# Context before tokens at the ends of feed-forwards, a later silu, and GpSimd's sums of a gate on VectorE

## The reference

```python
for l in range(2):
    m  = (silu(c)     @ w_mod[l] + b_mod[l])      # 9 vectors of 1024: shift, scale, gate of three sublayers
    mc = (silu(c_ctx) @ w_mod[l] + b_mod[l])      # the same for the context
    x  = x  + 0.5 * m[2]  * swiglu(mod_norm(x,  m,  0), w1, w2)      # feed-forward "a", width 2816
    xc = xc + 0.5 * mc[2] * swiglu(mod_norm(xc, mc, 0), w1, w2)
    h, hc = mod_norm(x, m, 1), mod_norm(xc, mc, 1)
    # mixers: convolution, pooling, neighbourhood attention of h over itself and hc's keys and values;
    # in layer 0 hc is mixed too, in layer 1 only its keys and values are needed
    x = x + m[5] * (mixers(h, hc) @ w_out);  xc likewise in layer 0
    x = x + 0.5 * m[8] * swiglu(mod_norm(x, m, 2), w3, w4)           # feed-forward "b"; xc only in layer 0
return rms_norm(x, final_g)
# mod_norm(x, m, i) = rms_norm(x, g) * (1 + m[3i+1]) + m[3i]
# swiglu(h, w1, w2) = (silu(a) * b) @ w2 with a, b = split(h @ w1)
```

## Time and profile before

| | us |
|---|---|
| median of 3 runs | 3647.82 (3643.95 to 3649.64) |
| profiled execution, its own time | 3641.98 |
| its span, first to last instruction | 3640.1 |

### The profile page before, as it was taken

How to read it: one execution, slowest core, us unless ns; L and a number is a source line. 1 busy time by engine, 2 the same in 40 slices (tenths; PEclk the granted TensorE clock), 3 DMA queues, 4 the chain that set the end, 5 groups by cost and what they waited for, 6 DMA issues and landing times.

```text
span 3640.1 us, 45778 instructions
## 1 busy us (share of the span) xinstructions
PE 3329.7 (91%) x17814; PEld 2927.8 (80%) x17814; DVE 2582.4 (71%) x4566; ACT 1320.5 (36%) x2339; POOL 806.9 (22%) x773
## 2 busy tenths in 40 slices
PE   6989799998899997999789999878999979889998
PEld 4778678786899996877679999868999968778886
DVE  4476668786889887465598888878988863653333
ACT  3465442323333334334433333343333343332222
POOL 0000011112433330301063333234333303100000
PEclk9999999999999998999899999989999989999999
DMA  3201245462233332522113333222333324113332
GB/s 124 90 24 41 76 139 184 141 190 73 79 104 105 110 105 80 157 89 75 44 50 105 110 105 102 90 67 87 102 105 101 103 88 121 47 59 98 93 99 76
DMA packets 382857, 348.89 MB, mean 96 GB/s; under 512 B 17344, under 2 KB 338240, under 8 KB 382128
## 3 DMA queue, kind: packets, MB, share of 16 engines
q1 hardware_dynamic: 337600, 250.74, 22.8%
q10 hardware_dynamic: 29088, 52.57, 4.6%
q0 software_dynamic: 15952, 42.65, 3.9%
HBM read 339.60 MB, written 2.10 MB: 94 GB/s over the span
## 4 chain that ended last, share of the span: by engine, by line
PE 49%; DVE 36%; ACT 8%; issue 6%; DMA 1%; POOL 0%; ACTq 0%; DVEq 0%; SPq 0%; POOLq 0%
PE ps L765 47%; DVE lob L2242 5%; DVE Tm L2846 5%; DVE MRa L2265 5%; ACT hib L1507 3%; DVE MRb L2265 3%; DVE X L2416 2%; ACT Tm L1507 2%; DVE lob L2240 2%; PE ps L768 1%; DVE Tm L2355 1%; DVE Gla L2855 1%; DVE Hl L2366 1%; DVE C L2416 1%; DVE ACC L2332 1%
## 5 line engine op out<-in xcount | busy, mean ns | idle before, releaser
L765 PE MATMUL ps<-Hh,hib 128*128 128x512 f32 (+2 forms) x2624 | 959.1, 366 | 83.3 <-DVE lob L2242 42.7
L765 PE MATMUL ps<-Hl,hib 128*128 128x512 f32 (+2 forms) x2624 | 942.2, 359 | 0.0
L765 PE MATMUL ps<-Hh,lob 128*128 128x512 f32 (+2 forms) x2624 | 941.9, 359 | 0.0
L2240 DVE TENSOR_TENSOR lob<-rawb,hib 128x1024 fp32r<-128x1024 f32 (+3 forms) x355 | 437.2, 1235 | 474.1 <-ACT hib L1507 472.8
L1507 ACT ACTIVATE hib<-rawb 128x1024 fp32r<-128x1024 f32 (+2 forms) x595 | 510.4, 865 | 670.5 <-PE ps L765 542.0
L765 PEld LDWEIGHTS ps<-Hh,hib 128*128 128x128 f32 x2624 | 507.4, 193 | 161.5 <-DVE lob L2242 51.4
L765 PEld LDWEIGHTS ps<-Hh,lob 128*128 128x128 f32 x2624 | 506.7, 193 | 51.7
L765 PEld LDWEIGHTS ps<-Hl,hib 128*128 128x128 f32 x2624 | 508.0, 194 | 49.9 <-issue 2.0
L765 PE MATMUL ps<-Gha,hib 128*128 128x512 f32 (+1 forms) x704 | 243.0, 345 | 9.4 <-ACT Tm L1507 4.0
L2265 DVE CUSTOM_DVE_ANT_0 MRa<-MRa 128x512 f32<-128x512 f32 x256 | 249.0, 1017 | 0.0
L765 PE MATMUL ps<-Gha,lob 128*128 128x512 f32 (+1 forms) x704 | 241.1, 342 | 0.0
(11 more groups left out here) (314 smaller groups left out, 6233.9 us busy)
## 6 DMA issues: line engine op xcount, KB each, us to landing
rawb<-in_ffn_w_in SPq DMA_DIRECT2D x120, 512.0 KB, 3.9
rawb<-in_ffn_w_out SPq DMA_DIRECT2D x88, 512.0 KB, 3.4
rawb<-in_w_in SPq DMA_DIRECT2D x74, 512.0 KB, 3.7
rawb<-in_w_ff SPq DMA_DIRECT2D x64, 512.0 KB, 3.6
MRa<-in_w_mod_t ACTq DMA_DIRECT2D x128, 256.0 KB, 2.7
rawb<-in_ffn_w_in SPq DMA_DIRECT2D x112, 256.0 KB, 3.2
MR<-in_w_mod_t POOLq DMA_DIRECT2D x96, 256.0 KB, 3.4
MRb<-in_w_mod_t ACTq DMA_DIRECT2D x64, 256.0 KB, 2.7
```

The costliest lines, as they stand in the source:

```text
L765: return e.matmul(out, lhsT, rhs, start=start, stop=stop)
L2240: e.tensor_tensor(lob_of(x.chunk), raw_of(x.chunk), hib_of(x.chunk), ALU.subtract).then_inc(*done(("lo", x.u)))
```

## The change

- At a last part's end the context's four pairs come first, then the tokens'; the context's norm runs in turn beside the tokens' pairs, in groups 1, 1, 4, 4 (`NORM_BY_4`). `following` names the context's norm, and every `ffn` opens with the tokens' norm between. The weights' order follows (`residual`, `sweeps`).
- The mixers open with the context's values, in layer 0 its three convolution products too, and the tokens' norm runs in turn beside them (`NORM_OPENING`); the tokens' values and the keys come behind.
- For the token norms 0, 2, 3, 5, 6, 8, 9 (`alone`) DVE doesn't add the last two squares to ACC: PE sums them straight from Tm. DVE's X updates of a pair come before its sums. The diagonals are signalled, and spread, one by one.
- `silu(turn)` moves from the start of `ffn` to behind its first pair (DVE waits for it before a row).
- `seven`: ACT's copy of product 5 and POOL's two adds go; DVE makes `b1` and `b2` from `u` and product 5 in PSUM. The last gate and its high and low half (`gated a2`, `high a2`, `low a2`) are put behind the first units of the next pair, except in a part's last pair.
- Rows: turns of 56, 56, 58, 59, 59; three behind an output chunk, and one at position 4 of every second crossed pair. In ACT's `gemm` the halves come before the row DMAs.

```diff
-        for some in ([[s] for s in sets] if apart else [sets]):
+        for some in ([[s] for s in sets[::-1]] if apart else [sets]):
...
+        tm(("v2", l, "c"), w, 8, 2048, 512, 2)
         if l == 0:
             conv("c")
+        tm(("v2", l, "x"), w, 8, 2048, 512, 4)
+        for pair in range(2):
+            fm(("k2", l, pair), w, 8, [1536 + 256 * pair, 1664 + 256 * pair], ["x", "c"])
...
+def alone(s, n):
+
+    return s == "x" and n in (0, 2, 3, 5, 6, 8, 9)
...
 NORM_BY_4, NORM_BY_8 = (1, 1, 4, 4), (1, 1, 2, 2, 2, 2)
+NORM_OPENING = [(0, 1, 0, 1, 1, 1, 1, 1, 2, 2), (0, 1, 1, 2, 6)]
...
-        mod_turns = [(0, 0, 48, 2, 0), (0, 48, 48, 2, 0), (0, 96, 64, 2, 2), (1, 16, 64, 2, 2), (1, 80, 64, 2, 2)]
+        mod_turns = [(0, 0, 56, 2), (0, 56, 56, 2), (0, 112, 58, 3), (1, 26, 59, 3), (1, 85, 59, 3)]
...
                     for i in range(nt // 128):
-                        m = mm(ps[:, b, i:i + 1], ACC[:, t0 + 128 * i:t0 + 128 * i + 128], ones[:, 0:1], True, True)
-                    m.then_inc(*done(("rsum", name)))
+                        m = mm(ps[:, b, i:i + 1], ACC[:, t0 + 128 * i:t0 + 128 * i + 128], ones[:, 0:1],
+                               not own_sums or i == 0, not own_sums)
+                    for k in own_sums:
+                        w.wait_ge(*at("sqt", name, k))
+                        for i in range(4):
+                            m = mm(ps[:, b, i:i + 1], Tm[:, get("tmp", "sq", name, k)[0], 128 * i:128 * i + 128], ones[:, 0:1],
+                                   False, k == 7 and i == 3)
...
-                    if next_norm and some[0] == "x":
-                        in_turn(norm_steps(*next_norm))
+                    if next_norm and some[0] == "c":
+                        in_turn(grouped(norm_steps(*next_norm), NORM_BY_4))
...
 (tensor, near_mixers)
-                for s in ("x", "c"):
-                    whole(("v2", l, s), tm_products, tm_act(acts[s]), cnorm(l, 1) if s == "x" else None)
-                    give_all(("v2", l, s))
+                in_turn(grouped(norm_steps(*xnorm(l, 1)), NORM_OPENING[l]))
+                whole(("v2", l, "c"), tm_products, tm_act(acts["c"]))
+                give_all(("v2", l, "c"))
+                for stage in range(0 if l else 3):
+                    whole(("conv", l, "c", stage), fm_products, acts)
+                    give_all(("conv", l, "c", stage))
+                while later:
+                    run_later()
+                whole(("v2", l, "x"), tm_products, tm_act(acts["x"]))
...
 (scalar, gemm)
                 for c in rest:
+                    high_halves(reach(c))
                     mod_more()
-                    high_halves(reach(c))
...
 (scalar, ffn)
                     mod_more()
-                    silu(TURNS[N])
...
                         between = None
+                        if f == 0 and N in TURNS:
+                            silu(TURNS[N])
...
 (vector, residual)
-                            if final:
-                                square_in(norm[s], k, o, nt, t0)
+                        for n, s in P[key].outs if final else []:
+                            square_in(norm[s], 2 * pair + n, None, *((T, 0) if s == "x" else (TC, T)))
...
 (vector, seven)
+                    if left:
+                        left.pop(0)()
...
                     elif m == 5:
-                        tmp("seven", name, "b2")
-                        tmp("seven", name, "b1")
+                        tmp_mine("seven", name, "b1")
+                        own()
+                        add("b1", slot("u"), product(5))
                     elif m == 7:
-                        w.wait_ge(*at("b1", name))
-                        add("u", slot("u"), product(7), ("free", "o", name, 7), ("u3", name))
+                        add("u", slot("u"), product(7), ("free", "o", name, 7))
+                        tmp_mine("seven", name, "b2")
+                        own()
+                        add("b2", slot("u"), product(5), ("free", "o", name, 5))
...
                     else:
+
+                        tmp("seven", name, "a2")
+                        add("a2", slot("u"), product(4), ("free", "o", name, 4), ("whole", name, "a2"))
                         low("a1", 0)
-
-                        tmp("seven", name, "a2")
-                        w.wait_ge(*at("b2", name))
-                        add("a2", slot("u"), product(4), ("free", "o", name, 4), ("whole", name, "a2"))
-                        gated("a2", "b2")
-                        low("a2", 1, ("g", N, part, f))
-                    if pos in (1, 4) and not last:
+                        left[:] = [lambda: gated("a2", "b2"), lambda: low("a2", 1, ("g", N, part, f))]
+                        while last and left:
+                            left.pop(0)()
+                    if pos == 4 and f % 2 == 0:
                         mod_step(1)
...
 (gpsimd)
-                e.tensor_tensor(slot("b1"), slot("u"), slot("b2"), ALU.add).then_inc(*done(("b1", name)))
-                e.tensor_tensor(slot("b2"), slot("b2"), slot("u"), ALU.add).then_inc(*done(("b2", name)))
```

More of the change, by code:

```diff
@@ L2152, in near_mixers @@
                 if l == 0:
-                    for stage in range(3):
-                        whole(("conv", l, "c", stage))
                     whole(("pool", l, "c"))
@@ L3095, in near_mixers @@
                         *done(("free", "o", ("v2", l, "c"), i), ("vx", l, i)))
+                for stage in range(0 if l else 3):
+                    whole(("conv", l, "c", stage))
+                    conv_stage(l, "c", stage)
+                finish_later()
+                whole(("v2", l, "x"))
                 for pair in range(2):
@@ L3108, in near_mixers @@
                 if l == 0:
-                    for stage in range(3):
-                        whole(("conv", l, "c", stage))
-                        conv_stage(l, "c", stage)
                     whole(("pool", l, "c"))
```

115 lines of the change are left out of this document (55 added, 60 removed).

## The result

The changed kernel takes 3504.01 us (median of 4 runs, 3500.44 to 3507.09), the kernel before 3647.92 (4 runs): a ratio of 0.9607, 95% interval 0.959 to 0.9623, so 144 us less. The forecast was 3560 with a range of 3516 to 3608.

What follows compares the result with a forecast made beforehand. TensorE, busy 91% of the span, was taken as the bound, so gains must come from its idle 310 us. 23 + 30 + 7 + 11 + 28 - 2 - 9 = 88 us less gave 3560 us by the runs, range 3516 to 3608.

Steps and rivals of the forecast that it cites:

- Part 1: Feed-forward openings: silu behind the first pair shortens the wait for the diagonal; 23 us gained, 2 us charged.
- Part 5: Inside the feed-forwards: moved rows and gate sums relieve VectorE, so lob waits mostly go; 28 us gained, 9 charged.
- the 9 for output stages: Output stages: 9 us charged for VectorE's 2.7 us overrun, twelve times, row DMAs behind the half and a fuller first block.
- Parts 2 and 3: Feed-forward ends and mixers' start: context first at ends, then alone, gains 30 us; TensorE's higher clock there gains 7.
- the lag of 10.7 us: End of the first mixers: sums start 10.7 us behind the tokens' last matmuls because VectorE is behind.
- The wait behind the mask: Mixers' start: ScalarE's mask load and copy stand ahead of its next half; 6.4 us idle remains on TensorE.
- Part 4: Token norms: paired X updates and last two squares on TensorE save 1.4 or 2.2 us each time; 11 us.
- the signs: Expected trace marks: no context diagonal wait at mixers' start, lob under 15 us, row mean under 0.85, ends idle about 31.
- A: Rival, whole kernel: waits at the ends shrink to the mask's and no overrun shows; 125 us less, 3523; 12%.
- B: Rival, output stages: VectorE's 2.7 us overrun reaches TensorE twelve times and takes half the inner gain; 3597; 14%.
- D: Rival, output stages: 24 row operations collide with GpSimd as a rule, mean 1.25 us; slower, 3722; 4%.
- C: Rival, moved norm: VectorE's 10.7 us lag grows, so stream order and squares bring 19 us instead of 41; 3582; 12%.

## Why the prediction was wrong

**Part 1, silu (23, -2).** Right in mechanism: root within 4.0 us of the row DMAs, no wait over 3 us for the diagonal at an opening. The size of 23 us is right as a sum; by opening 5.2, 9.7 and 8.3 stand for 9, 6 and 8, so that two misses cancel, which is luck.

**Part 5, inside the feed-forwards (28, -9).** The step that failed. It is worth 71 us where I took 19; inside the feed-forwards the crossed parts alone gave 62.1. Three faults. (1) I summed the waits for lob, 43.2 us, and took two thirds, because VectorE still had 50.6 us of work in 63. All of it went: 42.3 us of PE's idle time in the crossed parts, 28.6 in the twelve later ones and 13.7 in the three first ones, which were 68.4, 67.6 and 67.5 us long and are now 60.8 to 61.1. (2) What a wait costs beyond its own length stood in no term of this part. The part of 62.1 us is 3.7 over 58.4 and shows 3.0 of idle time; the other 0.7 us is in PE's busy time, 59.1 instead of 58.4. Half of it is how the rows are drawn: matmuls follow each other at 0.17 us and each row is 0.33 long, so idle time starts only at the end of the last row, 0.16 late, at each of two stops. The other half is three longer steps, 0.28 us for 0.17. In parts with a clock of 0.97 it is 2 us, and there the granted clock was 0.50, the lower level of 1.2 GHz, for 2.7 us behind a stop of 2.6 (columns as in the earlier trace rows, kernel before):

```profile
2023.00:2025.70 2.70, 2.66 (x8) 2.66 (x9) 2.51 (x3) 2.00 (x5) 1.29 (x1) 0.50 0.65 201
```

Over all crossed parts this is 19.8 us. (3) As to the 9 for output stages: none showed, the stage is 33.7 us as before. I had 24 row operations in it and 4.3 us of collisions, 35.7 us of VectorE; they are 20 at 745 ns, 1.2 us of collisions, and VectorE is busy 29.9. So the 28 should have been 28 + 14.3 + 19.8 and the 9 nothing: 62.1.

**Parts 2 and 3, order and clock (30 + 7).** Too high. The order is worth 6 us. I had counted the waits at the ends, and the lag of 10.7 us with them, mostly as the order's; the lag was the squares' pace, as the sums' start in seven kernels shows. The wait behind the mask, which I had named as the one that would stay, did stay, at 6.5 and 6.7 us where 6.4 was worked out. The clock did rise at the ends (0.79 to 0.91, 0.76 to 0.94, 0.84 to 0.92). PE's busy time fell by 9.5 us in the three stages that hold them, near the 7 forecast, but that holds longer rows around stops too, and no run separates the two; whether 7 was right stays open.

**Part 4, squares (11).** Too low by 24 us: 1.4 us a pair is right (5.58 less 4.19), but it is gained on every pair of a stage in which VectorE sets the pace, not on two. That 30 + 11 = 41 is also what both measure together, 41, is chance: two errors of the same lag, put down to the wrong part. Of the signs, the wait at the mixers' start, the diagonal and the rows' mean in the output stage came out; PE's idle time at the ends was less than forecast (24.8 for 31), and lob's waits more (29.2 for under 15), since plain chunks had been left out of the sum.

**The rivals.** A (everything goes, 3523) was nearest in time and right that no overrun shows; it too stopped at 37 us inside. B and D (the output stage becomes VectorE's) are out: VectorE is busy 29.9 of 33.7 us there. C, a lag that only moves, was the rival for the order, and has some truth: the lag went with the squares, not with the order. The Trainium skill, page "SBUF — State Buffer", section "Who interferes with whom", has a VectorE instruction with two SBUF inputs contend with a GpSimd instruction that reads SBUF, over a port pair that is an exclusive lock. The trace agrees: here the adds with one PSUM input took 539 to 556 ns in all of 420, and the row operations, which read two SBUF tiles, up to 1793. D's mechanism is out: collisions are bounded by the number of GpSimd's operations, as I had set against it, so more rows don't bring more of them.

## What to carry to other kernels

Compare the length of repeated stages, not the sum of waits: a stage of 62.1 us whose matmuls need 58.4 has 3.7 to give, whatever the wait row says. Before calling an in-order engine's idle time slack, see which of its waits its own order forces (3.6 us of turns to ScalarE and back here), and what it did without a gap ahead of the wait that it causes; its busy time and waits added up come near the stage's length even where it is not the bound. Two edits that each lift the same surplus aren't additive, and undoing only one hides what they do. Where an engine must wait for another between two steps of a loop, issue both first steps before both second ones; that moved loop brought 35 us here, and the cleverer half of the same edit nothing that the runs can tell.

## What was not expected of the hardware

A stop of TensorE of 2.6 us cost the part 3.7 us together with a short one of 0.4, at a granted clock of 1.00; where the clock was at its lower level for 2.7 us behind the stop (0.97 over the part) it was 4.3 to 4.7. GpSimd's operations lengthen about as many of VectorE's, by 0.8 to 0.9 us each, and which ones hardly matters: with 18 of them in a part 17 VectorE operations were lengthened, with 10 to 12 it was 10 to 12, whether VectorE had 13 row operations there or 9.
